# The last step of a hybrid trunk layer: the scale vector g2 spread in two halves, and the upper output columns finished between the two halves of the last product

## The reference, cut to what matters

```
x = x + g1 * y                                         # after the token mixer
hn = rms_norm(x, norm2_w) * (1 + sc2) + sh2
gate = sigmoid-routed weights of the 8 chosen experts of each token
a = silu(hn @ w_gate[e]) * (hn @ w_up[e])              # per expert e, 256 columns
routed = sum over e of (a * gate[e]) @ w_down[e]       # 1024 columns
x = x + g2 * (routed + shared)                         # g2: one vector of 1024 per stream
```

## Time and profile before

| quantity | value |
|---|---|
| runs, median (lowest to highest) | 652.46 us (651.79 to 655.53) |
| the profiled execution | 652.59 us |
| its span in the trace | 650.8 us |
| TensorE busy | 582.6 us, 90% of the span |
| VectorE busy | 212.4 us, 33% |
| ScalarE busy | 167.3 us, 26% |
| GpSimd busy | 29.3 us, 5% |
| DMA, mean over the span | 388 GB/s |
| mean granted TensorE clock | 0.968 of full speed |

### The profile page before, as it was taken

One profiled execution on the slowest core, in us unless ns is written; L12 is line 12 of the kernel. 1 busy time (PEld: TensorE's weight loads), 2 busy tenths in 40 slices (PEclk: granted clock), 3 DMA queues, 4 the chain that ended last, 5 costly groups with the idle time before them and its releaser, 6 DMA issues.

```text
span 650.8 us, 11025 instructions
## 1 busy us (share of the span) xinstructions
PE 582.6 (90%) x4524; PEld 406.9 (63%) x4524; DVE 212.4 (33%) x474; ACT 167.3 (26%) x302; POOL 29.3 (5%) x75
## 2 busy tenths in 40 slices
PE   0789999999899999989999999687999999998583
PEld 0478777788767676657575766355567667674251
DVE  0296777788832212011222221020121212211103
ACT  3064626672622121112121212000112121221020
POOL 1240220010100000000000000000000000000000
PEclk9969999999999999999999999788999999998897
DMA  8999599979998999999999999999999999999992
GB/s 324 385 344 369 173 380 391 409 293 398 420 388 370 361 421 408 419 422 420 421 421 419 423 419 422 420 421 419 422 421 420 419 421 420 422 420 420 421 355 78
DMA packets 49288, 252.56 MB, mean 388 GB/s; under 512 B 5817, under 2 KB 9025, under 8 KB 24913
## 3 DMA queue, kind: packets, MB, share of 16 engines
q1 hardware_dynamic: 47008, 246.50, 93.5%
q0 software_dynamic: 1840, 4.21, 2.0%
q10 hardware_dynamic: 384, 1.08, 0.4%
HBM read 250.06 MB, written 1.72 MB: 387 GB/s over the span
## 4 chain that ended last, share of the span: by engine, by line
PE 62%; DMA 24%; ACT 4%; DVE 4%; SPq 3%; issue 3%; ACTq 0%; DVEq 0%
PE bank L1210 22%; PE bank L1252 11%; DMA spare<-in_w_up 6%; PE bank L1181 6%; PE bank L1226 5%; DMA xn<-in_w_up 4%; DMA gb<-in_w_down 4%; DMA ring<-in_w_up 4%; PE bank L808 3%; DMA ring<-in_w_in 3%; SPq L596 2%; DMA ring<-in_w_down 2%; PE bank L858 2%; PE bank L854 2%; PE bank L850 2%
## 5 line engine op out<-in xcount | busy, mean ns | idle before, releaser
L1210 PE MATMUL bank<-ring,xe 128*64 128x256 f32 (+1 forms) x1680 | 178.8, 396 | 23.6 <-DMA ring<-in_w_up 9.1
L1210 PEld LDWEIGHTS bank<-ring,xe 128*64 128x64 f32 (+1 forms) x1680 | 118.3, 131 | 79.1 <-issue 44.4
L1252 PE MATMUL bank<-ring,actT 128*64 128x512 f32 (+1 forms) x400 | 88.9, 631 | 7.1 <-DMA ring<-in_w_down 2.9
L2183 DVE TENSOR_TENSOR act_e<-bank,sil 128x256 f32<-128x256 f32 x26 | 11.0, 425 | 188.3 <-ACT sil L1622 188.3
L2194 DVE SCALAR_TENSOR_TENSOR ylo<-bank,gslot,yhi 128x512 fp32r<-128x512 f32 x52 | 39.1, 751 | 92.3 <-ACT yhi L1630 92.3
L1630 ACT ACTIVATE yhi<-bank,gslot 128x512 fp32r<-128x512 f32 x52 | 35.7, 687 | 125.8 <-PE bank L1252 125.8
L1622 ACT ACTIVATE sil<-bank 128x256 f32<-128x256 f32 x26 | 10.0, 385 | 192.7 <-PE bank L1210 192.7
L1252 PEld LDWEIGHTS bank<-ring,actT 128*64 128x64 f32 (+1 forms) x400 | 25.6, 132 | 44.9 <-issue 44.3
L1181 PE MATMUL bank<-pone,hhi 128*128 128x256 f32 x200 | 50.0, 288 | 0.0
L1181 PE MATMUL bank<-pone,hlo 128*128 128x256 f32 x200 | 48.9, 282 | 0.0
L1226 PE MATMUL bank<-yhi,ptone 128*128 128x512 f32 x104 | 44.1, 424 | 0.4 <-DVE ylo L2194 0.4
(11 more groups left out here) (348 smaller groups left out, 766.4 us busy)
## 6 DMA issues: line engine op xcount, KB each, us to landing
ring<-in_w_gate SPq DMA_DIRECT2D x55, 1024.0 KB, 24.2
ring<-in_w_up SPq DMA_DIRECT2D x50, 1024.0 KB, 25.7
ring<-in_w_down SPq DMA_DIRECT2D x46, 1024.0 KB, 25.8
ring<-in_w_mod SPq DMA_DIRECT2D x12, 2048.0 KB, 13.1
ring<-in_w_in SPq DMA_DIRECT2D x5, 2048.0 KB, 17.6
gb<-in_w_down SPq DMA_DIRECT2D x7, 1024.0 KB, 25.9
gb<-in_w_up SPq DMA_DIRECT2D x5, 1024.0 KB, 21.3
xn<-in_w_gate SPq DMA_DIRECT2D x5, 1024.0 KB, 17.3
```

Source lines behind the costliest of these rows:

```text
L1210: ins = mm(bank[6][j * w:(j + 1) * w, part * FE:(part + 1) * FE], xe[:, k, slots], weights[:, k, :], start=(k == 0), stop=(k == KD - 1))
L1252: ins = mm(bank[4 + h][j * w:(j + 1) * w, :], actT[:, f, j * w:(j + 1) * w], weights[:, f, 512 * h:512 * h + 512], start=(f == 0), stop=(f ...
```

## The change

`spread_g2` becomes a function of the column half. The upper half (n = 1, banks 4 and 5) is spread where the whole was spread before, behind the gate products. The lower half (n = 0, banks 7 and 6) is spread behind the upper half of the last down product. Behind it, still ahead of the lower half of the last down product, stands now the combine of the upper columns. On VectorE `finish(0, 0)` moves from behind the last `ylo` to ahead of it, and on ScalarE the two copies of the lower half of g2 stand behind the first of the last two `yhi`. In the lower columns, too, the residual of stream 1 is now added by GpSimd. The fence shows the edits; the passing on of the flag `ends` in ScalarE's and VectorE's `pair` and `two_steps` is left out.

```diff
+        G2_BANKS = ((7, 6), (4, 5))
...
             def add_residual(turn):
-                w = slice(512, 1024)
-                pool.wait_ge(scaled, 4 * turn + 1)
-                pool.tensor_tensor(outb[:, 1, w], outb[:, 1, w], xt[:, 1, w], ALU.add).then_inc(final_ready[0][1], 1)
+                for i, w in enumerate((slice(512, 1024), slice(0, 512))):
+                    pool.wait_ge(scaled, 4 * turn + 2 * i + 1)
+                    pool.tensor_tensor(outb[:, 1, w], outb[:, 1, w], xt[:, 1, w], ALU.add).then_inc(final_ready[i][1], 1)
...
-            def spread_g2():
+            def spread_g2(n):
                 row = MODS.index("g2")
-                for q, (s, n) in enumerate(((0, 0), (0, 1), (1, 0), (1, 1))):
-                    if q == 3:
-                        pe.wait_ge(g2_kept, 1)
-                    ps = bank[(7, 4, 5, 7)[q]]
+                for s in range(NST):
+                    ps = bank[G2_BANKS[n][s]]
...
                         pe.wait_ge(y_lo, n * 2)
-                        spread_g2()
+                        spread_g2(1)
...
                         pe.wait_ge(a_copied, n + 1)
                         if ends:
-                            pe.wait_ge(g2_kept, 3)
+                            pe.wait_ge(g2_kept, 2)
...
                     ins.then_inc(y_filled, 1)
+                    if ends and i == 0:
+                        spread_g2(0)
+                        combine(1, n, final=True, halves=(0,))
...
-                combine(1, STEPS - 1, final=True)
+                combine(1, STEPS - 1, final=True, halves=(1,))
...
                     A(yhi[:, n, :], bank[4 + n][:, :], ACT.Copy, scale=gslot[:, par:par + 1]).then_inc(y_hi, 1)
+                    if ends and i == 0:
+                        keep_g2(0, NST)
...
                                            in1=yhi[:, n, :].bitcast(F32), op0=ALU.mult, op1=ALU.subtract).then_inc(y_lo, 1)
+                    if ends and i == 0:
+                        finish(0, 0)
...
             def finish(turn, i):
                 w = halves[i]
-                dve.wait_ge(g2_kept, 4)
+                dve.wait_ge(g2_kept, 2 * i + 2)
...
-                for s in ((0,) if i == 0 else (1, 0)):
+                for s in (0,):
...
             first_round()
-            for i in range(2):
-                finish(0, i)
+            finish(0, 1)
```

More of the change, by code:

```diff
@@ L1618, in gathered, with pair @@
                       ACT.Copy).then_inc(x_copied, 1)
-            def pair(par, n_pair, group, last=False, starts=False):
+            def pair(par, n_pair, group, last=False, starts=False, ends=False):
                 act.wait_ge(e_filled, n_pair + 1)
@@ L1635, in shared_gate, with keep_g2 @@
                 A(ssil[:, 1, :], bank[7][:, NST * P:2 * NST * P], ACT.Silu).then_inc(sg_copied, 1)
[L1637 to L1641, removed]
+            def keep_g2(n, first):
+                for s in range(NST):
+                    act.wait_ge(g2_spread, first + s + 1)
+                    A(gb[:, s, 512 * n:512 * n + 512], bank[G2_BANKS[n][s]][:, :], ACT.Copy).then_inc(g2_kept, 1)
             def two_steps(n, group, last=False, shared=False, starts=False, ends=False):
@@ L1647, in two_steps @@
                 if ends:
-                    keep_g2()
-                pair(1, n + 1, group, last)
+                    keep_g2(1, 0)
+                pair(1, n + 1, group, last, ends=ends)
             def first_round():
@@ L2178, in turned, with pair @@
                 ins.then_inc(t_copied, 1)
-            def pair(kind, par, e, n_pair, following, starts=False):
+            def pair(kind, par, e, n_pair, following, starts=False, ends=False):
                 dve.wait_ge(e_silu, n_pair + 1)
@@ L2199, in pair, with two_steps @@
                     one_hots(following, e + 2 * kind, posm_s)
-            def two_steps(kind, e, n, following, starts=False, shared=False):
+            def two_steps(kind, e, n, following, starts=False, shared=False, ends=False):
                 pair(kind, 0, e, n, following, starts)
@@ L2204, in two_steps @@
                     shared_act()
-                pair(kind, 1, e, n + 1, following)
+                pair(kind, 1, e, n + 1, following, ends=ends)
             def shared_act():
@@ L2221, in first_round @@
                         two_steps(PAIR, 24 * it + 16 + 4 * i, 10 * it + 6 + 2 * i, PAIR if i < 3 else QUAD)
-                two_steps(QUAD, NE - 8, STEPS - 2, None)
+                two_steps(QUAD, NE - 8, STEPS - 2, None, ends=True)
             def later_round(r):
```

## The result

The changed kernel takes 650.34 us (median of 20 runs, 648.26 to 652.04) against 651.62 us (20 runs, 649.81 to 655.53): the ratio is 0.9971, with a 95% interval of 0.996 to 0.9983, which is 1.9 us less (1.1 to 2.6). Run twice more beside other runs of the kernel before, it gave 0.9972 (0.9955 to 0.9989) and 0.9969 (0.9952 to 0.9986). It is faster, by a third of a percent.

What follows compares the result with a forecast made beforehand. The last stretch was taken as bound by its chain behind the last w_down landing, fixed at about 636.5. The last add moves from 646.44 to 645.8, -0.6: 652.59 becomes 652.0, and 651.8 as median; range 649.7 to 653.8.

Steps and rivals of the forecast that it cites:

- The point: Whole kernel: 0.6 us less than the profiled execution, with 651.8 us predicted as the median.
- the forecast: Last stretch: the clock's fall moves from the lower down product to up, -0.6 us; chance 0.50.
- the first rival: Up and lower down product: the clock holds in both, -2.3 us, so 650.3; chance 0.30.
- the clock's price ahead of up: Up product: the longer idle gap makes the clock fall, costing 1.69 us, within bounds of 0 to 1.69.
- The gap ahead of up: TensorE before up: moving half the spread away makes it idle for 3.06 us instead of 1.20.
- The Trainium skill's rule: TensorE ahead of up: long idle gaps halve the clock; with the rule 652.0 us, without it 650.3.
- The work between the down halves: TensorE between the last down halves: 1.86 of spread plus 0.94 of combine, 2.80 us where it idled 2.90.
- The second rival: Up, then lower down product and combine: the clock falls twice, +1.4 us, so 654.0; chance 0.15.
- VectorE's order: VectorE, upper finish ahead of the last ylo: lower finish starts at 643.2 instead of 643.96, -0.7 us.
- a delay of 0.2: VectorE's last ylo: queued behind the upper finish, it starts about 0.2 us late, at 641.1.
- GpSimd: Lower finish: GpSimd's residual add is no help, 2.58 us against 2.48, +0.10.

Runs made afterwards that it cites:

- the gap filled: Changed kernel plus four products nobody reads behind the first half of the spread, ahead of up: 0.9959 of before; with yhi products ahead of ylo products too, 0.9957.
- the whole spread ahead with yhi first: Changed kernel, but all of g2 spread ahead of up as before, and yhi products ahead of ylo products in the last combines: 0.9947 of before.
- the upper finish back: Changed kernel with VectorE's finish of the upper columns behind the last ylo again: 0.9997 of before, 0.9988 when run again.
- the yhi products first: Changed kernel with the two yhi products of each last combine ahead of the two ylo products, the ylo wait between them: 0.9953 of before.

## Why the prediction was right, point by point

*The direction and the range held, the size was low.* The point said 0.6 us less; measured is 1.9 (1.1 to 2.6), by the medians 1.3. That lies between the forecast and the first rival (2.3), and the traces say why: both occur. Of the three traces of the changed kernel two went as the forecast (0.79 less than before from up to the last add) and one as the rival (2.09 less). The step that failed is the one that took the clock's price ahead of up as 1.69 in every execution. It is 1.69 in some and 0 in others, so its mean is below the value I put into the sum: the mean of the three traces is 1.2 less.

Where up falls, the two distances account for the 0.79: the lower product starts 12.38 behind the start of up instead of 10.81, and what is behind it is 2.36 shorter. Where up keeps its clock, it starts 11.10 behind, since the landing came that much later in this trace, and what is behind it is 2.38 shorter: 2.09.

*The gap ahead of up.* I computed 3.06 from the gate product's 5.35. Over the eight traces that have the changed gap unfilled it was 1.74, 2.02, 2.19 and 2.26 with up at 3.66, and 2.70, 2.71, 2.92 and 3.03 with up at 5.16 to 5.35. The short ones all stand behind a gate product of 5.86 to 6.32: where more of gate runs at the lower clock, it ends later, and the gap shrinks, since the start of up lies 9.97 to 10.23 behind the start of gate in all eight. I had taken gate's end as fixed, and the first rival put a shorter gap down to an earlier landing of w_up. In the changed kernel's first trace that was not the cause: up starts 10.23 behind gate there, and 10.20 before.

*The Trainium skill's rule* against idle gaps ("TensorE: Matmul & The Clock Gate", section "Why this matters for your kernels") agrees with these eight traces: up fell behind the four longer gaps and not behind the four shorter ones, and in the two traces with the gap filled it stayed at 3.66. It does not cover every fall: in the whole spread ahead with yhi first, the clock fell in the lower product with no gap above 0.81 between the halves. The cost of up's fall at the end was 1.3 (19.86 less 18.56), not 1.69, since the wait of 0.33 for the last landing takes up most of the rest; in the pair with the upper finish back it was 1.57 (20.85 less 19.28).

*The work between the down halves.* Forecast 2.80, measured 2.78 where up is late, and the clock held in the lower product. The second rival (a second fall, slower than before) showed in none of the changed kernel's traces. That the clock can fall there without a long gap ahead, which it rests on, the combination just named does show.

*VectorE's order.* Forecast -0.7 in the sum (643.96 against 643.2); the experiment gives 0.99 with the clock the same in both. Part of the difference is a delay of 0.2 that I gave to the last ylo behind the upper finish: in the changed kernel's second trace ylo starts at 640.52, 0.03 behind the end of yhi. This is most of why the picture that I forecast ended 0.79 and not 0.6 earlier.

*GpSimd.* Forecast +0.10, measured +0.10 (7.48 against 7.38, the changed kernel's second trace against the one with both adds on VectorE).

*The bookkeeping closes:* from the lower product to the last add, 1.50 of clock + 0.99 of VectorE's order - 0.10 of GpSimd's add = 2.39, and 9.84 - 7.46 = 2.38 was measured.

What stays open is how often each kernel loses its clock, and where. There is one trace of the kernel before, and it lost it in the lower product; if other executions do not, the mean gain of the change is less than these differences say.

## What to carry to other kernels

When a stretch ends on a transfer's landing, put into the wait before it whatever the later chain would queue behind: here the finish of the first half, which held VectorE for 1.04 us when the second half was ready. Work moved from one wait to another also moves an idle gap, and on TensorE the clock can follow it, so compute both gaps and not only the one that gets filled. And where a wait covers two inputs, order the work by which of them comes first: that gave 0.53 us here for no new instruction.

## What the runs showed of the hardware

I had not expected that the same program shows two pictures of the same stage, with gate and up at 6.04 and 3.66 in one execution and at 5.35 and 5.35 in another. Nor does the gap's length alone tell what the clock does: ahead of up it held behind 2.26, but in the down product one step earlier it fell behind a gap of 2.06, and in the kernel with the yhi products first even behind 1.65, with a mean clock of 0.68 over the 5.29 us of products behind it. And a fall came in the lower product behind no more than 0.81 and 0.74, where in another trace the clock held behind 1.69 and 0.60. What decides in these cases the runs do not show.
